# Layer boundaries of a diffusion-style transformer: sums of both norms gathered during the output tiles, per-token factors in columns, four tiles led side by side

## What is computed

```python
def rms_norm(x, g):
    y = x * rsqrt(mean(x * x, axis=-1) + EPS)
    return y * g

def first_block(x, c, ctx, ...):            # DEPTH = 2
    for l in range(DEPTH):
        last = l == DEPTH - 1
        h  = rms_norm(x,  norm_pre[l]) * (1 + sc) + sh
        hc = rms_norm(xc, norm_pre[l]) * (1 + scc) + shc
        z, zc = h @ w_in[l], hc @ (w_in[l][:, :COL_Q] if last else w_in[l])
        # attention (rotated q and k), long convolution, gated MLP, then:
        out = merge_branches(z, (y_a, y_b, y_c), w_branch[l], w_out[l])   # ... @ w_out
        x_new = x + gt * rms_norm(out, norm_post[l])
        if not last:
            xc = xc + gtc * rms_norm(outc, norm_post[l])
        x = x_new
    return x
```

## Time and profile before

| | |
|---|---|
| Runs | 1448.44, 1451.06, 1453.69 us; median 1451.06 |
| Profiled execution | span 1448.2 us from the first to the last instruction; no time of its own is listed beside the span |
| Mean granted TensorE clock | 0.984 |
| PE busy | 1391.8 us, 96% of the span |
| DVE busy | 923.0 us, 64% |
| ACT busy | 689.0 us, 48% |
| POOL busy | 41.8 us, 3% |
| HBM | 139 GB/s over the span |

### The profile page before, as it was taken

How to read it: one execution, slowest core, us unless ns; L and a number is a source line. 1 busy time by engine, 2 the same in 40 slices (tenths; PEclk the granted TensorE clock), 3 DMA queues, 4 the chain that set the end, 5 groups by cost and what they waited for, 6 DMA issues and landing times.

```text
span 1448.2 us, 20966 instructions
## 1 busy us (share of the span) xinstructions
PE 1391.8 (96%) x8380; PEld 1176.7 (81%) x8380; DVE 923.0 (64%) x1625; ACT 689.0 (48%) x1190; POOL 41.8 (3%) x50
## 2 busy tenths in 40 slices
PE   5999999999999999989999999988999999999998
PEld 2577668777888888669888899987988999888888
DVE  5555764776523444388775777657667777888546
ACT  5333544234322232555356454455556746666444
POOL 0000000000000000100000000010000002000001
PEclk9999999999999999999999999998999999999999
DMA  9321343144332232623234455554543345655552
GB/s 369 134 89 58 145 160 117 44 154 161 104 113 87 87 102 75 226 70 99 77 119 143 137 177 190 184 166 126 183 145 112 95 145 176 200 188 194 191 174 74
DMA packets 57794, 202.36 MB, mean 140 GB/s; under 512 B 6272, under 2 KB 9536, under 8 KB 57696
## 3 DMA queue, kind: packets, MB, share of 16 engines
q1 hardware_dynamic: 55568, 194.01, 40.3%
q0 software_dynamic: 1760, 6.25, 1.3%
q10 hardware_dynamic: 368, 0.74, 0.2%
HBM read 199.93 MB, written 1.05 MB: 139 GB/s over the span
## 4 chain that ended last, share of the span: by engine, by line
PE 88%; DVE 8%; ACT 3%; DMA 1%; issue 1%; ACTq 0%; DVEq 0%; SPq 0%
PE gemm_bank L415 17%; PE gemm_bank L417 16%; PE gemm_bank L416 16%; PE misc_bank L415 4%; PE misc_bank L416 4%; PE misc_bank L417 4%; PE misc_bank L426 3%; PE gemm_bank L426 3%; PE gemm_bank L571 1%; PE misc_bank L571 1%; PE misc_bank L427 1%; PE gemm_bank L427 1%; PE misc_bank L823 1%; PE gemm_bank L504 1%; PE misc_bank L864 1%; DVE wlo L1729 1%
## 5 line engine op out<-in xcount | busy, mean ns | idle before, releaser
L1729 DVE TENSOR_TENSOR wlo<-raw,whi 128x1024 fp32r<-128x1024 f32 x316 | 382.8, 1223 | 75.5 <-ACT whi L1208 71.9
L1208 ACT ACTIVATE whi<-raw 128x1024 fp32r<-128x1024 f32 x316 | 332.7, 1055 | 168.9 <-PE gemm_bank L417 101.5
L415 PE MATMUL gemm_bank<-halves,wlo 128*128 128x256 f32 (+1 forms) x1152 | 375.3, 326 | 19.1 <-DVE halves L2192 5.9
L417 PE MATMUL gemm_bank<-halves,whi 128*128 128x256 f32 (+1 forms) x1152 | 360.1, 313 | 0.0
L416 PE MATMUL gemm_bank<-halves,whi 128*128 128x256 f32 (+1 forms) x1152 | 360.0, 312 | 0.0
L415 PEld LDWEIGHTS gemm_bank<-halves,wlo 128*128 128x128 f32 x1152 | 222.5, 193 | 43.4 <-issue 18.8
L417 PEld LDWEIGHTS gemm_bank<-halves,whi 128*128 128x128 f32 x1152 | 222.8, 193 | 12.1
L416 PEld LDWEIGHTS gemm_bank<-halves,whi 128*128 128x128 f32 x1152 | 223.2, 194 | 11.2 <-issue 0.7
L415 PE MATMUL gemm_bank<-arena_r,wlo 128*128 128x512 f32 (+1 forms) x320 | 108.3, 338 | 0.5 <-DVE wlo L1729 0.5
L417 PE MATMUL gemm_bank<-arena_r,whi 128*128 128x512 f32 (+1 forms) x320 | 107.6, 336 | 0.0
L416 PE MATMUL gemm_bank<-arena_r,whi 128*128 128x512 f32 (+1 forms) x320 | 107.6, 336 | 0.0
(11 more groups left out here) (419 smaller groups left out, 2289.4 us busy)
## 6 DMA issues: line engine op xcount, KB each, us to landing
raw<-in_stream SPq DMA_DIRECT2D x348, 512.0 KB, 3.4
arena<-in_stream SPq DMA_DIRECT2D x16, 512.0 KB, 11.3
x<-in_x SPq DMA_DIRECT2D x1, 1024.0 KB, 6.3
x<-in_ctx SPq DMA_DIRECT2D x1, 1024.0 KB, 9.8
y<-in_hy_decay POOLq DMA_DIRECT2D x2, 512.0 KB, 4.5
arena<-in_gm_ws POOLq DMA_DIRECT2D x2, 512.0 KB, 5.4
const_b<-in_const_b POOLq DMA_DIRECT2D x1, 763.0 KB, 6.6
y<-in_hy_w POOLq DMA_DIRECT2D x2, 256.0 KB, 4.0
```

The costliest lines, as they stand in the source:

```text
L415: mm(out, w_lo, r_hi, start=first, stop=False)
L417: return mm(out, w_hi, r_hi, start=False, stop=last)
L1208: act.activation(self.whi[:, t % SPLIT, :], self.raw_tile(t), ACT.Copy).then_inc(*self.mark("tile_hi", "tile_hi", t))
L1729: dve.tensor_tensor(self.wlo[:, t % SPLIT, :], self.raw_tile(t), self.whi[:, t % SPLIT, :].bitcast(F32), ALU.subtract).then_inc(*self.mark ...
```

## The change

1. **Sums during the output tiles.** The mean square of the new `x` is taken from x + r·b (b the gated output, r the factor of the first norm) as mean(x²) + 2r·mean(x·b) + r²·mean(b²). For each output tile ACT also squares the gated output (`bsq`, one per half), DVE multiplies it with x and adds up (`xb`), POOL adds two sums (`pool_branch_sums`). The mean square of the input x is taken at the start (`pe_input_energy`).
2. **Columns.** `pe_norm_sums` and `pe_norm_last` are twelve matmuls of one column for each half, with tokens on the partitions. Root, reciprocal and the formula (`dve_cols`, `dve_energy`, `dve_norm_new`) work on 2 to 6 columns. `pe_norm_spread` brings the two factors back to rows in misc_bank3 and misc_bank0, and DVE reads them there.
3. **Rows one by one.** `dve_cross_rows` goes through the rows: scaled(k), sum(k-1), new(k), low half (k-2), with the other work in between.
4. **Filter transform of layer 1 in two parts**: the first before the queries, the second behind all keys; `act_kern(1, 1)` and the second `dve_kern` move into `act_block1` and `dve_block1`. The gemm bank that it borrowed is no longer borrowed.
5. **Order of the keys**: half 0 of all four, then half 1 of all four.
6. **Boundary 1**: `pe_last_quad` leads four tiles (zc0, zc1, head0, head1) side by side in the order `QUAD`.

```diff
-CROSS_KEYS = ((0, 0), (1, 0), (2, 0), (0, 1), (1, 1), (3, 0), (2, 1), (3, 1))
+CROSS_KEYS = ((0, 0), (1, 0), (2, 0), (3, 0), (0, 1), (1, 1), (2, 1), (3, 1))
...
+    def pe_norm_sums(self, l, s):
+
+        pe, (bank, c) = self.pe, self.norm_bank(s)
+        pe.wait_ge(*self.at("pooled", ("out", l), KT - 2))
+        pe.wait_ge(*self.at("xb_sum", l, KT - 2))
+        for a, src in enumerate(self.norm_sums(s)):
+            for e in range(2):
+                pe.matmul(bank[:, c + 4 * a + 2 * e:c + 4 * a + 2 * e + 1], src[:, e * P:(e + 1) * P], self.c["mean_all"][:, 0:1], start=True, stop=True)
...
+    def pe_norm_spread(self, l, s, i):
+
+        pe = self.pe
+        pe.wait_ge(*self.at("norm_r", l, s, i))
+        if s:
+            pe.wait_ge(*self.at("h", l + 1, 0, KT - 1))
...
     def pe_cross_queries(self, tiles):
...
-            if step in CROSS_SUMS:
-                self.pe_cross_sum(1, CROSS_SUMS.index(step))
+            if step == 2 * KT + 7:
+                for r in range(2):
+                    self.pe_norm_spread(0, 1, r)
...
-        for k in range(KT):
-            self.pe_cross_sum(0, k)
+        self.pe_norm_last(0, 0)
+        self.pe_norm_sums(0, 1)
+        self.pe_norm_spread(0, 0, 0)
+        self.pe_norm_last(0, 1)
+        self.pe_norm_spread(0, 0, 1)
+        self.pe_spec(1, 0, 1)
         self.pe_cross_queries(queries)
         for i, side in CROSS_KEYS:
             self.pe_cross_keys(keys[i], side, (i, side) == (0, 1))
+        self.pe_spec(1, 1, 2)
         self.pe_next += 8
...
-        pe.wait_ge(*self.at("rstd", ("res", 1)))
-        self.pe_tiles(2)
-        self.pe_heads(3)
+        self.pe_last_quad()
+        self.pe_tiles(1)
+        for n in range(2):
+            self.pe_head(n)
...
         if l:
             self.act_tiles(1, split=False)
+            self.act_kern(1, 1)
             self.act_tiles(4)
...
+    def dve_cross_rows(self, s):
+
+        v = self.dve
+        v.wait_ge(*self.at("spread_r", 0, s, 0))
+        for k in range(KT + 2):
             if k < KT:
+                self.dve_scaled(0, s, k)
+            if s == 0 and k == 1:
+                self.dve_cols(0, 1)
+            if k == 1:
+                v.wait_ge(*self.at("spread_r", 0, s, 1))
+            if 1 <= k <= KT:
+                self.dve_cross_sum(s, k - 1)
+            if k < KT:
+                self.dve_new(0, s, k)
+            if k >= 2:
+                self.dve_cross_lo(s, k - 2)
+            if s == 0 and k in (3, 5):
+                (self.dve_energy if k == 3 else self.dve_norm_new)(0, 1)
+            if s == 0 and k == 6:
+                self.dve_tap_rs(1)
+            if s == 0 and k == 2 or s and k in (0, 1, 2, 3):
                 self.dve_lo()
```

More of the change, by code:

```diff
@@ L213, in plan @@
     return tiles, extra
-POOLED = (("out", 0), ("out", 1), "g_ffn")
+POOLED = ("g_ffn",)
 class Kernel:
@@ L1583, in act_block1 @@
             return
[L1584 to L1587 removed]
+        self.act_norm_out(1, 0)
+        self.act_hi()
+        self.act_norm_new(1, 0)
     def act_pair(self, which, z):
@@ L1802, in dve_tile @@
                 self.dve_half("g_ffn", j - 1, 1)
+        elif kind == "wout":
+            acc, to = self.both_halves(7, 1, n), self.both_halves(5 if j else 7, 1, n)
+            if j >= 2:
+                dve.wait_ge(*self.at("xb_sum", l, j - 1))
+            if j < KT - 1:
+                dve.wait_ge(*self.at("branch", l, j, n // TOK - 1))
+                self.own(dve.tensor_tensor(to, self.both_halves(j, 0, n), self.by_half(self.x[:, j, 0:n], n), ALU.mult))
+                if j:
+                    dve.tensor_tensor(acc, acc, to, ALU.add).then_inc(*self.mark("dve_norm", "xb_sum", l, j))
+            else:
+                for s in range(n // TOK):
+                    dve.wait_ge(*self.at("branch", l, j, s))
+                    dve.tensor_tensor(self.piece(5, s), self.branch_out(j, s), self.x[:, j, self.half(s)], ALU.mult).then_inc(*self.mark("dve_norm", "xb", l, j, s))
         elif kind == "ffg":
@@ L2327, in dve_block1 @@
             return
-        self.dve_rstd(("out", l), n)
-        for k in range(KT):
-            out = self.branch_out(k, 0)
-            self.own(v.tensor_tensor(out, out, self.tmp[:, 2, 0:n], ALU.mult))
-            v.tensor_tensor(self.x[:, k, 0:n], self.x[:, k, 0:n], out, ALU.add).then_inc(*self.mark("dve_x", "x_new", l, k))
     def dve_compress(self, which):
```

291 lines of the change are left out of this document (184 added, 107 removed).

## The result

The changed kernel takes **1496.45 us** (1494.51 to 1497.07, 4 runs) against 1450.38 (1448.44 to 1453.69, 4 runs): ratio 1.0319, 95% interval 1.0301 to 1.0336, 3.2% slower. The direction is the forecast's, the size is not: +46 us measured, +17 forecast, 1475 the end of the range. Its profiled execution spans 1495.8 us at a mean clock of 0.969.

The account below looks back on a forecast made before the run. PE was 88% of the chain, so time changes only where PE waits or gains work. Boundary 0 +18.4, boundary 1 -1.2, output tiles and input energy 0: +17.2 on the median gave 1468 us, range 1456 to 1475.

Parts of the forecast that it names:

- Boundary 0 behind the first query: First layer boundary, queries to attention: late evacuations delay keys by 11.0 us, the late value tile adds 7.4 us.
- wait on the evacuation: Boundary 0, first key matmul: PE stands 11.4 us until ACT evacuates the first query tile from the shared PSUM bank.
- a turn of the ring: Boundary 0 keys: rounding, low half, scaled row, sum and h hand over between ACT and DVE, 3.6 us a turn.
- the +18.4: Boundary 0: the attention starts at 729.4 against 710.98, 18.4 us later.
- The output tiles themselves: Output tiles and input energy: added work hides under PE's own tile time, cost 0 for both.
- Second boundary: Behind layer 1's output tiles: a gain of 1.2 us, reduced because DVE and GpSimd run about 1.5 us late.
- gains between 2 us and nothing: Boundary 0, first query matmul: comes up to 2 us sooner; 1 us was taken.
- The SBUF rule: Boundary 1: two-input DVE and GpSimd instructions reading SBUF block each other throughout, making DVE about 1.5 us late.
- No bank wait: Rival at boundary 0: no PE gap from ring and queue, only the late value tile stays; +5.8, 1457 us, chance 0.07.
- The short norm wins: Rival at both boundaries: DVE is not late, first low half 9.2 us behind the last output matmul; 1443, chance 0.07.
- The loss is taken back behind the attention: Rival behind the attention: a stage where PE waits for weights absorbs the loss; 0 to +4, 1453, chance 0.06.
- +11 to +22 with -4.5 to +1.5: Bounds in us on the time change: the first pair for boundary 0, the second for boundary 1.

Follow-up runs that it names:

- e2_evac: Changed kernel with each query bank evacuated right behind the rounding of the same-numbered key tile at boundary 0, not all four behind the ring; 1486.2 us, ratio 1.0261.
- e3_kern: Changed kernel with ACT's copy of the second transform part behind the second value tile's rounding and DVE's use behind two low halves; 1493.32 us, ratio 1.0305.
- e4_xb: Changed kernel with DVE's product and sum of each layer 0 output tile behind the next weight tile's low half, not ahead; 1485.18 us, ratio 1.0246.
- e1_quad_wait: Changed kernel with TensorE's three waits for GpSimd-started transfers behind the four side-by-side tiles and the fifth, not ahead of them; 1482.24 us, ratio 1.0228.
- h1_bound1_wait: Kernel before with the change at boundary 1 only, TensorE's three transfer waits placed behind the fifth tile; median 1447.42 us, ratio 0.9994.
- h0_bound1: Kernel before with the change at boundary 1 only, TensorE's three transfer waits still ahead of the tiles; 1461.03 us, ratio 1.0078.
- e9_spread: Changed kernel with five order edits, half 0's spreads ahead of half 1's column sums at boundary 0, and the first transform part among the queries; ratio 1.0063.
- e6_pool: Changed kernel with GpSimd's second sum cut to 8 columns for output tiles 2 to 6 of both layers; 1496.61 us, ratio 1.0324.

## Why the prediction was right in direction and wrong in size

**Boundary 0 behind the first query: right.** The steps and what they measured: wait on the evacuation 11.4 forecast, 10.8 measured; the low clock behind it 2.7 us forecast, 1.5 measured (eight key halves in 24.7 us instead of 23.2); a turn of the ring 3.6 and 3.47; gap before the first value matmul "near 3", 2.89; from the first query to the first scores 85.7 (643.7 to 729.4) and 84.7. e2_evac removes the first cause and e3_kern the second. From the first query to the first scores the forecast has 19.4 us more than the 66.3 of before (the +18.4, and the 1 us that was to be won ahead of it), and 18.4 were measured: this is the term of the sum that stood.

**"The output tiles themselves ... Both 0; the cover is PE's own tile time": wrong, 12.0 us.** This is one of the two steps that failed. I compared busy times with the length of a tile, and the busy time is indeed covered: with the same work in another order (e4_xb) the stretch takes 54.5 us, against 54.1 before and 66.1 in the changed kernel. Of the 12.0 us, 7.8 are waits of PE for low halves and the rest is what the clock lost behind them, which my sum had for the two boundaries only. What counts is what stands behind the waiting instruction. The product waits for the evacuation of a tile, and the low half of the next tile, which had nothing to do with it, is queued behind. The trace of before showed why this place is delicate, in rows that I had read and did not use (timeline of the kernel before, ACT and PE):

```profile
585.50 1.06 ACT L1208 ACTIVATE whi<-raw 128x1024 fp32r<-128x1024 f32 x1 [4.83 <-DMA raw<-in_stream]
...
606.02 1.06 ACT L1208 ACTIVATE whi<-raw 128x1024 fp32r<-128x1024 f32 x1 [3.88 <-DMA raw<-in_stream]
...
587.87 0.50 PE L415 MATMUL gemm_bank<-arena_r,wlo 128*128 128x512 f32 x1 [0.52 <-DVE wlo L1729]
```

ACT waits here for raw tiles to land, and PE already waits for a low half: the ring had no slack left.

**"Second boundary ... I take -1.2": wrong, +7.8 to the first tile.** The other step. The columns and rows came about as worked out: the columns' end 2.7 us behind the last product, first low half 11.2 us behind the last output matmul, against 9.1 forecast for a DVE that is free and 1.5 more allowed for one that is not; with GpSimd's second sum cut short it was 9.3. But I followed the four engines and left out the transfers that GpSimd starts behind the last row of x, and PE's wait for them, although row order is just what the change moves. With that wait out of the way the boundary gains 1.9 us to the first compress matmul in e1_quad_wait and h1_bound1_wait, and between 0.3 and 3.0 us in all five profiles: my -1.2 lies among them. In h0_bound1 the loss stands alone, 9.9 us to the first compress matmul.

**First query, "gains between 2 us and nothing": wrong by 4.4 us** (3.4 lost where 1 was to be won). This is a term mis-sized. Counted from the last output matmul's end, DVE was through with the taps at 5.7 us, as forecast (5.4). PE's one-column matmuls then ran at half clock, 1.85 us for eight rows where the earlier trace rows have 0.95, and ended at 10.2 instead of 7.8. From there to the first scaled row it took 3.7 us instead of 2.3, and from that row to the first low half 5.6 instead of 3.9, because half 1's columns stand ahead of half 0's spreads; DVE waited 3.5 us in three waits for PE there (1.51, 1.07 and 0.89):

```profile
644.41 1.85 PE L675 MATMUL misc_bank<-const_a,halves_f 128*128 128x1 f32 x8
...
652.62 1.85 PE L675 MATMUL misc_bank<-const_a,halves_f 128*128 128x1 f32 x8
654.32 1.20 PE L694 MATMUL misc_bank<-const_a,norm_r 128*128 128x128 f32 x4
...
655.63 0.42 DVE L2365 TENSOR_TENSOR halves_f<-halves_f,misc_bank 128x256 f32<-128x256 f32 x1 [1.51 <-PE misc_bank L694]
```

The first low half ended 19.5 us behind the last output matmul; I had 14.0, and 16.3 as the bound at half clock (644.8), which was too low as well. e9_spread took the spreads out of that queue, and its time did not fall.

**The SBUF rule** of the Trainium skill ("SBUF — State Buffer", "Who interferes with whom") again fits the durations, 3.44 us for two low halves beside GpSimd's 2.33 and 2.25. Of the 1.5 us that I charged for it at boundary 1 nothing could be seen in e6_pool's time, but its profile has the first low half 2.0 us sooner there. That reading a row's factor from PSUM adds nothing came out as forecast: scaling a row from misc_bank takes 0.40 to 0.42 us, and adding it to x, from SBUF alone, 0.42.

**Rivals.** "No bank wait" is excluded by the 10.8 us row. "The short norm wins" fell at both places. "The loss is taken back behind the attention" fell too: 35.1 us late at the scores, 35.9 at layer 1's last output matmul. The range did not hold since both failed steps were of a kind that had no case in it: work that could have run, queued behind a wait that had nothing to do with it. Its ends were also not quite what the bounds give: +11 to +22 with -4.5 to +1.5 is +6.5 to +23.5, from 1457.6 to 1474.6 us, so 1456 to 1475 is no cut at either end. The last 3.3 us, behind the compress matmuls, stay open: e1_quad_wait has 0.1 there, h0_bound1 1.7, h1_bound1_wait -1.4, so they may be nothing but the difference of two executions. The same holds for single stretches in general: the changed kernel's code up to layer 0's last output matmul ended at 641.75, and in e1_quad_wait and e3_kern, with the same code there, at 638.8; 2 to 3 us of that difference stand already at the last row of layer 0's merge (575.6 against 573.7 and 572.7).

## What to carry to other kernels

Added work under another engine's time is free only if nothing of use is queued behind its wait: for each new wait, list the next instruction on that engine, ask whether it needed to wait, and put the new work behind it. That mattered most where the weights' ring was already waiting for transfers. When the order of rows changes, look at everything that is released by the last row, transfers on other queues too, and place each wait for them directly ahead of its first use: here the same boundary was 8 to 10 us slower by the profiles with the waits ahead of five tiles, and 0.3 to 3 us faster with them behind, a gain that the times could not show.

## What the runs showed of the hardware

A stretch of one-column matmuls did not bring TensorE's clock back. In the changed kernel PE waits 1.98 us behind the last output matmul (641.75), the granted clock falls from 1.00 to 0.50 at 644.3, and the windows behind it are (columns as in the earlier trace rows):

```profile
646.00:654.00 8.00, 6.78 (x33) 6.70 (x32) 3.72 (x11) 1.54 (x3) 0.00 (x0) 0.50 0.37 130
654.00:661.00 7.00, 7.00 (x26) 5.79 (x26) 3.50 (x11) 1.41 (x4) 0.00 (x0) 0.50 0.00 0
661.00:664.00 3.00, 1.39 (x6) 0.60 (x5) 2.96 (x8) 1.16 (x3) 0.00 (x0) 0.94 0.18 37
```

PE is recorded as busy for 13.8 of 15 us, mostly with products of one column, and has 1.2 GHz throughout. It came back to 2.4 GHz at 661.3, after 2.6 us of the first transform's products, which are 512 columns wide. The small products, being at half clock, took about twice as long: 0.46 us instead of 0.24 each. In the kernel before, the eight rows of L675 stood between sums of 512 columns and took 0.95 us.
